# One-hot matmuls for the last two expert pairs' rows, and the rows' factors found before the first rows are used

## The reference, cut to what matters

```python
t = rmsnorm(x, norm2_g)                     # 576 tokens x 1024
g_sel = argmax(t @ w_group)                 # 1 of 4 groups
top_p, top_i = top_k(softmax(el_sel), 2)    # 2 of the 8 experts of that group
w = p_sel * top_p / sum(top_p)
for e in range(32):
    a = silu(t @ w_gate[e]) * (t @ w_up[e])          # 1024 x 256 each
    out = out + comb[:, e:e+1] * (a @ w_down[e])     # 256 x 1024
return x + out
```

## Time and profile before

| | |
|---|---|
| median of 3 runs | 609.05 us |
| the three runs | 616.21, 608.38, 609.05 us |
| the profiled execution | 614.63 us, of which the span from first to last instruction is 612.8 us |
| TensorE busy | 513.2 us, 84% of the span |
| VectorE, ScalarE, GpSimd busy | 40%, 24%, 25% |
| HBM read, written | 138.16 MB, 17.83 MB |
| longest parts of the chain that ended last | PE 48%, SP's queue 14%, DVE 13%, DMA 9% |

### The profile page before, as it was taken

The page is one execution under the profiler, slowest core; times in us unless marked ns, Lnnn a source line. Parts: engine busy times, 40 slices in busy tenths (PEclk is TensorE's granted clock), DMA queues, the critical chain, the costliest instruction groups (busy, mean ns, idle before and its releaser), DMA issues.

```text
span 612.8 us, 7846 instructions
## 1 busy us (share of the span) xinstructions
PE 513.2 (84%) x2918; PEld 320.3 (52%) x2918; DVE 244.4 (40%) x569; ACT 144.3 (24%) x363; POOL 151.7 (25%) x288
## 2 busy tenths in 40 slices
PE   2596999899999999889993498999978687879671
PEld 2584766677776777567782353343423233333231
DVE  2856768758431455641227303222111111111037
ACT  3553353444535223122001101110100000000010
POOL 4164745103304454633002201112111111000000
PEclk9888999799999899999996598999979899898897
DMA  8521040022015902266818689999999999999574
GB/s 244 199 72 34 14 138 2 2 70 70 2 63 200 317 22 71 71 241 239 343 70 345 286 322 390 350 421 425 425 421 425 427 426 424 425 425 420 214 262 154
DMA packets 34599, 145.05 MB, mean 237 GB/s; under 512 B 5849, under 2 KB 9001, under 8 KB 22272
## 3 DMA queue, kind: packets, MB, share of 16 engines
q1 hardware_dynamic: 26864, 131.58, 54.8%
q0 software_dynamic: 4672, 9.31, 4.2%
q10 hardware_dynamic: 3024, 3.64, 1.8%
HBM read 138.16 MB, written 17.83 MB: 255 GB/s over the span
## 4 chain that ended last, share of the span: by engine, by line
PE 48%; SPq 14%; DVE 13%; DMA 9%; issue 5%; ACT 4%; POOL 2%; ACTq 0%; DVEq 0%; POOLq 0%
PE banks L934 19%; SPq L646 10%; PE banks L1156 8%; DMA w_moe_b<-in_w_up_dram 5%; PE banks L1171 4%; SPq L654 4%; PE banks L992 2%; PE banks L1150 1%; DMA y_d<-y_sb,idx 1%; POOL w_lo L789 1%; PE banks L1109 1%; PE banks L1077 1%; PE banks L1233 1%; PE banks L1072 1%; DVE h_a L1621 1%
## 5 line engine op out<-in xcount | busy, mean ns | idle before, releaser
L789 POOL TENSOR_TENSOR w_lo<-w_raw,w_hi 128x512 fp32r<-128x512 f32 x52 | 69.0, 1344 | 128.2 <-ACT w_hi L1383 126.6
L1156 PE MATMUL banks<-w_moe_a,xgT 128*64 128x512 f32 x256 | 77.9, 643 | 11.8 <-DMA w_moe_a<-in_w_up_dram 11.8
L1156 PE MATMUL banks<-w_moe_b,xgT 128*64 128x512 f32 x224 | 70.7, 648 | 17.3 <-DMA w_moe_b<-in_w_up_dram 10.4
L934 PE MATMUL banks<-w_hi,xT_hi_a 128*128 128x512 f32 (+4 forms) x140 | 57.6, 411 | 7.0 <-ACT sv L1351 7.0
L835 POOL DMA_INDIRECT y_d<-y_sb,idx x15 | 15.1, 1009 | 171.4 <-PE banks L1150 112.5
L934 PE MATMUL banks<-w_lo,xT_hi_a 128*128 128x512 f32 (+4 forms) x140 | 54.9, 392 | 0.0
L934 PE MATMUL banks<-w_hi,xT_lo_a 128*128 128x512 f32 (+4 forms) x140 | 54.6, 390 | 0.0
L1962 DVE SCALAR_TENSOR_TENSOR glu<-banks,wr,glu 128x256 f32<-128x256 f32 x15 | 7.2, 483 | 115.7 <-ACT glu L1512 115.7
L1156 PEld LDWEIGHTS banks<-w_moe_b,xgT 128*64 128x64 f32 x224 | 22.4, 149 | 58.0 <-issue 57.5
L1156 PEld LDWEIGHTS banks<-w_moe_a,xgT 128*64 128x64 f32 x256 | 24.8, 148 | 39.4 <-issue 37.1
L1512 ACT ACTIVATE glu<-banks,wr 128x256 f32<-128x256 f32 x15 | 7.1, 473 | 157.0 <-PE banks L1156 129.5
(11 more groups left out here) (269 smaller groups left out, 855.4 us busy)
## 6 DMA issues: line engine op xcount, KB each, us to landing
w_moe_a<-in_w_down_dram SPq DMA_DIRECT2D x20, 1024.0 KB, 24.7
w_moe_a<-in_w_gate_dram SPq DMA_DIRECT2D x18, 1024.0 KB, 24.6
w_moe_a<-in_w_up_dram SPq DMA_DIRECT2D x18, 1024.0 KB, 28.0
w_moe_b<-in_w_gate_dram SPq DMA_DIRECT2D x14, 1024.0 KB, 12.5
w_moe_b<-in_w_up_dram SPq DMA_DIRECT2D x14, 1024.0 KB, 15.4
w_moe_b<-in_w_down_dram SPq DMA_DIRECT2D x12, 1024.0 KB, 17.5
w_raw<-in_w_in_dram SPq DMA_DIRECT2D x36, 256.0 KB, 4.3
y_d<-in_consts_dram SPq DMA_DIRECT2D x9, 512.0 KB, 10.0
```

Source lines behind the costliest of these rows:

```text
L789: nc.gpsimd.tensor_tensor(w_lo[:, s, :], w_raw[:, s, :], w_hi[:, s, :].bitcast(F32), ALU.subtract).then_inc(split, 1)
L934: l = mm(acc2[0:R, j % 2, 0:width], a[:, P * t:P * t + R], w, start=(kk == 0 and q == 0), stop=(kk == KD - 1 and q == 2))
L1156: l = mm(acc[64 * e:64 * e + 64, u, :].rearrange("p (m f) -> p m f", m=2), xgT[:, xu, k, 64 * e:64 * e + 64], units(at_e[e], 2)[:, :, k * ...
```

## The change

Four things are done:

1. `find_rows` for the factors (with its wait for `wr_ready`) goes on TensorE ahead of `rows_T` of pair 0. On VectorE `rows_in(0)` goes behind the seven steps that end in `pair_wr`.
2. Pair 14 is put to tokens like pair 15: `down_last(0)`, high parts on ScalarE, low parts on VectorE, a second set of `oh_last`. Its `pair_out` and `scatter` fall away.
3. SyncE's read of `y_d` waits for 7 scatters on each of the two semaphores (the last is pair 13's) instead of 8 and 7 (the last is pair 14's). `y_last` and `oh_last` lie in the ring's units 12 to 14 instead of 14 and 15.
4. TensorE's order at the end: `gate_up_of(15)`, pair 14's rows for tile 0, `act_T_of(15)`, pair 14's rows for tile 1, `down_last(1)`, `second_row(0)`, pair 14's rows for tile 2, pair 15's for tile 0; then `second_row` and pair 15's rows for tiles 1 and 2; then both pairs' rows for tiles 3 and 4. `last_rows` of one pair and tile is now four matmuls (two halves, high and low).

```diff
-YOUT = [16 * (NPAIR // 2), 16 * (NPAIR // 2 - 1)]
+YOUT = [16 * (NPAIR // 2 - 1)] * 2
...
@@ gpsimd
-            for p in range(LAST):
+            for p in range(LAST - 1):
                 if p + 4 < NPAIR:
                     gather(p + 4)
                 scatter(p)
@@ tensor
+            def down_last(q):
+                p = LAST - 1 + q
+                pe.wait_ge(aT_ev, p + 1)
+                pe.wait_ge(dn_in[p % 4], p // 4 * 32 + 32)
+                if q:
+                    pe.wait_ge(yl_hi, 2)
+                    pe.wait_ge(yl_lo, 2)
+                else:
+                    pe.wait_ge(y_ev, p)
...
+            def last_rows(i, q, first=False, final=False):
+                R = out_rows(i)
+                for n in range(2):
+                    pe.wait_ge(yl_hi, 2 * q + n + 1)
+                    pe.wait_ge(yl_lo, 2 * q + n + 1)
+                    bank, cols = banks[0:R, FIN_BANKS[i] + n, :], slice(n * 512, n * 512 + 512)
+                    mm(bank, oh_last[:, q, i, 0:R], y_last[:, q, 0, cols], start=first, stop=False)
+                    l = mm(bank, oh_last[:, q, i, 0:R], y_last[:, q, 1, cols], start=False, stop=final)
+                if final:
+                    l.then_inc(fin_ps, 1)
...
+            pe.wait_ge(wr_ready, 1)
+            find_rows(32, pair_wr, row_oh.bitcast(F32)).then_inc(wr_ps, 1)
             rows_of_pair(0)
...
             gate_up_of(1)
-            pe.wait_ge(wr_ready, 1)
-            find_rows(32, pair_wr, row_oh.bitcast(F32)).then_inc(wr_ps, 1)
             rows_of_pair(2)
...
-            down_of(LAST - 1)
+            down_last(0)
...
             gate_up_of(LAST)
+            pe.wait_ge(oh_fin, 1)
+            last_rows(0, 0, first=True)
+            act_T_of(LAST)
+            last_rows(1, 0, first=True)
+            down_last(1)
             second_row(0)
-            act_T_of(LAST)
-            down_last()
-            for i in range(1, PE_ROWS):
+            last_rows(2, 0, first=True)
+            last_rows(0, 1, final=True)
+            for i in (1, 2):
                 second_row(i)
...
+                last_rows(i, 1, final=True)
             for i in (3, 4):
                 if i == 4:
                     pe.wait_ge(y_fin, 1)
...
+                last_rows(i, 0, first=True)
+                last_rows(i, 1, final=True)
@@ scalar
-            pair_out(LAST - 1)
+            def highs(q):
+                for n in range(2):
+                    act.wait_ge(y_ps, LAST + 2 * q + n)
+                    nc.scalar.copy(y_last[:, q, 0, n * 512:n * 512 + 512], acc[:, 2 + n, :]).then_inc(yl_hi, 1)
+
+            highs(0)
...
             pair_exp(LAST)
...
+            highs(1)
@@ vector
             step(nc.vector.memset(level0[:, :], 0.0))
-            rows_in(0)
             dve.wait_ge(r_expd, 1)
...
+            rows_in(0)
             rows_in(1, acc[:, 2:4, :])
             dve.wait_ge(wr_ps, 1)
...
+                    for q in range(2):
+                        for t in range(NT):
+                            l = stt(out=oh_last[:, q, t, :], in0=iota, scalar=float(P * t - 1),
+                                    in1=small[:, 152 + q:153 + q].to_broadcast([P, P]), op0=ALU.add, op1=ALU.is_equal)
                     l.then_inc(oh_fin, 1)
+            lows(0)
...
             for t in range(2):
                 row_in(t, 0)
-            for n in range(2):
-                dve.wait_ge(yl_hi, n + 1)
-                tt(y_last[:, 1, n * 512:n * 512 + 512], acc[:, 2 + n, :],
-                   y_last[:, 0, n * 512:n * 512 + 512].bitcast(F32), ALU.subtract).then_inc(yl_lo, 1)
+            lows(1)
             sums_in(0)
```

More of the change, by code:

```diff
@@ L1252, in _ @@
             with pe.If(n_most > CAP):
-                pe.wait_ge(y_ev, LAST)
+                pe.wait_ge(yl_hi, 2)
+                pe.wait_ge(yl_lo, 2)
                 pe.sem_inc(L_xt, 1)
@@ L1278, in second_row @@
                 for n in range(2):
-                    mm(banks[:, FIN_BANKS[i] + n, :], ident, y_tok(i, 1)[:, n * 512:n * 512 + 512], start=True, stop=False)
+                    mm(banks[:, FIN_BANKS[i] + n, :], ident, y_tok(i, 1)[:, n * 512:n * 512 + 512], start=False, stop=False)
             gate_up_of(LAST)
+            pe.wait_ge(oh_fin, 1)
[3 more added lines that the diff above has]
+            down_last(1)
             second_row(0)
-            act_T_of(LAST)
-            down_last()
-            for i in range(1, PE_ROWS):
+            last_rows(2, 0, first=True)
+            last_rows(0, 1, final=True)
+            for i in (1, 2):
                 second_row(i)
-            pe.wait_ge(oh_fin, 1)
-            for n in range(2):
-                for i in range(3):
-                    l = last_rows(i, i, n)
-                    if n:
-                        l.then_inc(fin_ps, 1)
+                last_rows(i, 1, final=True)
             for i in (3, 4):
@@ L1540, in _ @@
             pair_exp(LAST)
-            for n in range(2):
-                act.wait_ge(y_ps, NPAIR + n)
-                nc.scalar.copy(y_last[:, 0, n * 512:n * 512 + 512], acc[:, 2 + n, :]).then_inc(yl_hi, 1)
+            highs(1)
         @block.vector
@@ L1993, in _, with lows @@
                 if p == LAST - 1:
-                    step(nc.vector.tensor_copy(small[:, 156:157], idx[:, LAST:NPAIR]))
-                    for t in range(NT):
-                        l = stt(out=oh_last[:, t, :], in0=iota, scalar=float(P * t - 1),
-                                in1=small[:, 156:157].to_broadcast([P, P]), op0=ALU.add, op1=ALU.is_equal)
-                    l.then_inc(oh_fin, 1)
+                    step(nc.vector.tensor_copy(small[:, 152:154], idx[:, LAST - 1:NPAIR]))
+                    for q in range(2):
+                        for t in range(NT):
+                            l = stt(out=oh_last[:, q, t, :], in0=iota, scalar=float(P * t - 1),
+                                    in1=small[:, 152 + q:153 + q].to_broadcast([P, P]), op0=ALU.add, op1=ALU.is_equal)
+                    l.then_inc(oh_fin, 1)
+            def lows(q):
+                for n in range(2):
+                    cols = slice(n * 512, n * 512 + 512)
+                    dve.wait_ge(yl_hi, 2 * q + n + 1)
+                    tt(y_last[:, q, 1, cols], acc[:, 2 + n, :], y_last[:, q, 0, cols].bitcast(F32), ALU.subtract
+                       ).then_inc(yl_lo, 1)
+            lows(0)
             def row_in(t, k):
```

25 lines of the change are left out of this document (7 added, 18 removed).

## The result

| | before | after |
|---|---|---|
| median of 20 runs | 612.25 us (608.29 to 616.78) | 607.29 us (604.46 to 612.21) |
| ratio after / before, 95% interval | | 0.9929 [0.9905, 0.9952] |
| the profiled execution | 614.63 us (span 612.8) | 604.46 us (span 602.7) |

The change makes the kernel 0.7% faster, 4.3 us by the ratio, less than the 2% at which the forecast's chances divide. The forecast was 600.8 us, 8.3 us less than before, with a range up to 605.0 us. The way was right, the size about twice too large, and the measured time lies above the range.

What follows compares the result with a forecast made beforehand. The weights' DMA stream bounds the long middle, so only its start and the kernel's end can pay. Start 4.0 - 0.3 = 3.7 us plus end 4.6 gives 8.3; 609.05 - 8.3 = 600.8 us, range 596.8 to 605.0.

Steps and rivals of the forecast that it cites:

- the 2% at which the forecast's chances divide: Whole kernel, 12.2 us: faster than 596.9 us chance 0.10, slower than 621.2 us 0.03, between 0.87.
- the new wait: VectorE's tail: `sums_in(1)` waits for another `second_row` and four matmuls on TensorE, 0.3 us late.
- the last part: From the first `sums_in` to the end: a span beyond 12.4 us would show the forecast wrong.
- The rival "slower": TensorE's clock stays at half through the end after waiting for the last weights: 614.5 us, chance 0.05.
- The head, 0.3 us: Experts' start: ten float32 matmuls ahead of pair 0's `rows_T` cost 0 to 1.3 us, taken as 0.3.
- The stream, 4.0 us: Weights' DMA stream from 365 to 410 us: loads asked for 4.8 us sooner regain 4.0 us.
- its first rival: Stream regains little, clock stays low in pair 0's down, or head 1.3 us late: 602.5 to 604.5 us, chance 0.2.
- part 1: Experts' start: factors found earlier, ahead of pair 0's `rows_T`; 4.0 us regained less 0.3 gives 3.7 us.
- The end, 4.6 us: After pair 15's gate and up: new order starts `sums_in(0)` 4.9 us earlier, less 0.3, gives 4.6 us.
- The baseline: Whole kernel before: median taken as 609.05 us, from which the 8.3 us gain was subtracted.
- theory B: From the experiments, not the prediction: nothing is taken back; one profiled execution's waits misstate the kernel before.

Runs made afterwards that it cites:

- e5: The changed kernel with four VectorE operations moved behind the seven steps, so the factors' `find_rows` starts earlier: 606.85 us, ratio 0.9925 to the kernel before.
- e1: The kernel before with only the factors' part of the change (`find_rows` earlier), the end as before: 611.26 us, ratio 0.9991.
- e12: The kernel before with only the factors' part of the change, repeated on another chip: 610.78 us, ratio 0.9984.
- e3: The changed kernel without further edit, run beside its parts on one chip: 607.47 us, ratio 0.9949 to the kernel before.
- e8: The changed kernel without further edit, repeated on a second chip: ratio 0.9960 to the kernel before.
- e2: The kernel before with only the end's part of the change (points 2 to 4), the head as before: 609.54 us, ratio 0.9959.
- e9: The kernel before with gate and up weights of pair 15's second expert loaded only to a quarter: ratio 1.0008.
- e13: The kernel before without edit, one more profiled execution on yet another chip: 612.06 us.
- e7: The kernel before without edit, repeated on a second chip: ratio 1.0018.
- e11: The changed kernel with four VectorE operations moved behind the seven steps and VectorE's row additions at the end reordered into waits: 604.22 us, ratio 0.9878 to before.
- e16: The kernel before without edit, one more profiled execution on yet another chip: 607.86 us.

## Why the prediction was right in kind and wrong in size

**What held.** The factors' `find_rows` lies in the wait ahead of `rows_T`, all but 1.0 us of it; down of pair 0 runs at full clock; the stream has no hole; pair 13's scatter lands in 8.9 us (forecast 9.0) and the reads are waited for by nobody; 10.4 us from gate and up of pair 15 to the first `sums_in` (10.1), the new wait 0.35 us (0.3), the last part 12.3 us (at most 12.4). The rival "slower" did not come: down of pair 15 takes 3.65 us, at the 2.4 GHz level.

**The head, 0.3 us.** It costs 0.9 to 1.0, near its upper bound of 1.3. The forecast gave half weight to a clock that rises earlier behind the earlier work, by which the head would cost nothing. That did not happen: the granted clock is 0.50 up to T0 + 14 in before and after alike and 1.00 from T0 + 16 on in both. By the trace about half of the loss arrives at the end of the stream (e5).

**The stream, 4.0 us.** Against the execution shown, 3.0 us came back (236.95 to 233.95), with the head's loss in them, so 3.7 is the figure to compare. The step from rates to time was thus sized at most a little high. The larger miss is that these 3 us are not lost in every execution: the mean start of pair 15's gate and up is T0 + 236.2 over the seven of before, and T0 + 234.3 over five with the new head (e1, e12, after, e3, e8), so 1.9 us on the whole; the timing says 0.8 with 1.4 either way. The forecast did name the clock in this stretch, but took the 5.35 us of one execution for the kernel's. What it had under its first rival (part 1 gives 0 to 2 us) is what happened, though for another reason than any given there: not that the stream regains little, but that it had less to regain.

**The end, 4.6 us.** This is the step of the prediction that failed most: it took off the whole 15.1 us, with 3.2 us in it for which `second_row(0)` waited in one execution, as if the kernel paid them each time; over seven executions this wait is 1.6 us, from none to 3.2. The forecast followed one chain, through pair 14's scatter and the read, and measured the new order from the end of gate and up of pair 15. In this frame it was right to 0.3 us. But 15.1 us was the old distance in the one execution in which the `y_d` chain was latest; by the mean of seven the whole end shrinks by 2.8 us, and e2 timed 2.5. The step left out is the question of how far the second chain, that of the last weights, was behind the first. e9 answers it: before, 3.7 us of the last weights can be left out and nothing is gained. The waits answer it too: in five executions of seven the `y_d` chain is later, by 1.3 to 3.2 us, in e13 by 0.1, and in e7 that of the weights is.

**The baseline.** The 609.05 us were a median of three, 3.2 us under that of twenty. Taken off 612.25, the forecast's 8.3 us would have given 603.95 us. Of the 6.5 us between forecast and result, 3.2 are the baseline and 3.3 the terms (8.3 against 4.96 between the two medians), both in the same direction. That the three runs lay low, and the profiled one high, is chance and no fault of the mechanism; but even with the right median the forecast would have been 3.3 us too low.

**The sum with measured terms.** 1.9 us for the stream (the head's loss is in it) and 2.8 us for the end make 4.7 us, against 4.3 us by the main comparison and 2.4 to 3.1 us by e8 and e3. From the table: VectorE's end is T0 + 270.7 in the mean of seven before and T0 + 266.1 in that of three after, 4.5 us. The three comparisons of the whole change give 3.3 us in the mean. So theory B accounts for most of the shortfall: 3.6 us of the 8.3 by the terms. Between the 4.5 to 4.7 us of the profiles and the 3.3 us of the timings something over 1 us is left, within their intervals of 1.4 to 1.9 us. Two of the three profiles of the changed kernel are also faster than the median of their runs, by 2.8 and 1.4 us. That nothing at all is taken back is thus not shown, and two more things are open. In e8 TensorE keeps step with e3 up to T0 + 95, and the next weights come 1.9 us later (gate and up at T0 + 98.38 against 96.48), though the DMA engines are as busy as in e3 (424 GB/s from T0 + 73 to T0 + 98). SyncE issues its loads 1.3 us later from T0 + 81 on; what lies behind this wasn't found; whether such losses are commoner with the new head, three profiles can't say. And the share of executions of before that keep their clock is known only as two of nine.

## What to carry to other kernels

A wait read from one profiled execution is the price in this execution: before a change worth under 1% is priced, look at several, from a common point of the program, and use the mean. Of a wait to be removed ask how far the next chain is behind it; test this by shortening the other chain: if that gains nothing, the other one is not the later of the two, and the wait in several traces says by how much. When a transfer stream is full, asking for it earlier gives little more (0.6 us for 3 here), and what is left to win is behind it: in work on the engine that ends last, which can be put into its waits (e11).

## What the runs showed of the hardware that was not expected

The granted clock of TensorE can fall, or not, at the same instruction of the same kernel, behind the same waits (1.15 and 0.96 us in e13 and in e16). With the new head there is one wait of 1.41 us ahead of down of pair 0 instead of these two, and the clock fell in none of ten profiles. One such fall costs 1.7 us in the matmuls and 3 us at the end of the stream 200 us later. And the part ahead of T0, which no edit touched, differed by up to 5 us from one execution to the next, more than the change is worth.
